# Two merges and a convolution norm as one stage of sixteen weight tiles, and a feed-forward as one written-out stage

## What is computed

```python
y_a = a.reshape(B, S, ATTN_WIDTH) @ w_proj_attn[l]
c = jax.nn.silu(layer_norm(c, conv_ln_w[l], conv_ln_b[l]))
y_b = c @ w_proj_conv[l]
g_a, g_b = jnp.split(jax.nn.sigmoid(g + gate_b[l]), 2, axis=-1)
x = x + (g_a * y_a + g_b * y_b) @ w_out[l]
h = rms_norm(x, ffn_norm_w[l])
gt, up = jnp.split(h @ w_gate_up[l], 2, axis=-1)
x = x + (jax.nn.silu(gt) * up) @ w_down[l]
```

## Time and profile before

| What | Value |
|---|---|
| three runs | 3345.98 us median, 3337.95 to 3349.73 |
| profiled execution | 3353.64 us, its span 3351.9 us (1.7 us lie around the span) |
| mean granted TensorE clock | 0.947 of 2.4 GHz |
| PE busy | 2962.7 us, 88% |
| PEld busy | 2385.1 us, 71% |
| DVE, ACT, POOL busy | 1561.5, 1235.2, 736.0 us |
| moved | 218.90 MB, mean 65 GB/s |
| median time from issue to landing, 512 KB | 3.8 us (`w_raw`) to 5.1 us (`gates`) |

### The profile page before, as it was taken

The page is one execution under the profiler, slowest core; times in us unless marked ns, Lnnn a source line. Parts: engine busy times, 40 slices in busy tenths (PEclk is TensorE's granted clock), DMA queues, the critical chain, the costliest instruction groups (busy, mean ns, idle before and its releaser), DMA issues. The chain is left out here.

```text
span 3351.9 us, 34912 instructions
## 1 busy us (share of the span) xinstructions
PE 2962.7 (88%) x13448; PEld 2385.1 (71%) x13448; DVE 1561.5 (47%) x1927; ACT 1235.2 (37%) x2024; POOL 736.0 (22%) x323
## 2 busy tenths in 40 slices
PE   6999998877778989988998999694889989998998
PEld 5787887666667767776777778482677877787786
DVE  3666552346764337777878777514322111121121
ACT  3455442334542335555554554423224111111110
POOL 2111111100002322332233323112223212121111
PEclk7999999989989989999999999897999999999999
DMA  4111122131224212121112212241330111111112
GB/s 112 44 45 57 53 68 76 30 63 40 57 79 158 84 55 68 46 65 50 54 46 65 63 53 82 106 131 58 126 126 26 44 44 38 50 50 38 44 44 76
DMA packets 239270, 218.90 MB, mean 65 GB/s; under 512 B 29304, under 2 KB 200856, under 8 KB 239128
## 3 DMA queue, kind: packets, MB, share of 16 engines
q1 hardware_dynamic: 238096, 215.41, 21.0%
q10 hardware_dynamic: 1032, 1.57, 0.3%
HBM read 156.66 MB, written 41.42 MB: 59 GB/s over the span
## 5 line engine op out<-in xcount | busy, mean ns | idle before, releaser
L179 POOL TENSOR_TENSOR w_lo<-w_raw,w_hi 128x1024 fp32r<-128x1024 f32 (+3 forms) x220 | 521.1, 2371 | 2014.1 <-ACT w_hi L171 2014.1
L171 ACT ACTIVATE w_hi<-w_raw 128x1024 fp32r<-128x1024 f32 (+3 forms) x220 | 215.3, 983 | 666.5 <-PE u_y_ps L1688 221.3
L209 PE MATMUL d_pp<-h_hi,w_hi 128*128 128x512 f32 x896 | 367.9, 411 | 32.5 <-DVE d_padded L2523 20.7
L2501 DVE SCALAR_TENSOR_TENSOR d_acc<-d_padded,vectors,d_acc 128x1024 f32<-128x1024 f32 x240 | 388.3, 1618 | 3.6
L209 PE MATMUL d_pp<-h_hi,w_lo 128*128 128x512 f32 x896 | 366.2, 409 | 0.0
L209 PE MATMUL d_pp<-h_lo,w_hi 128*128 128x512 f32 x896 | 363.4, 406 | 0.0
L209 PEld LDWEIGHTS d_pp<-h_hi,w_hi 128*128 128x128 f32 x896 | 173.2, 193 | 80.2 <-issue 25.4
L209 PE MATMUL s_pp<-h_hi,w_hi 128*128 128x512 f32 x512 | 206.8, 404 | 13.1 <-PEq L67 13.1
L2281 POOL TENSOR_TENSOR d_probs<-d_probs 128x128 f32<-128x128 f32 (+3 forms) x64 | 129.5, 2024 | 385.8 <-ACT d_probs L2397 385.8
L209 PE MATMUL s_pp<-h_hi,w_lo 128*128 128x512 f32 x512 | 205.2, 401 | 0.0
L209 PE MATMUL s_pp<-h_lo,w_hi 128*128 128x512 f32 x512 | 204.2, 399 | 0.0
(11 more groups left out here) (346 smaller groups left out, 6542.7 us busy)
## 6 DMA issues: line engine op xcount, KB each, us to landing
w_raw<-in_w_in SPq DMA_DIRECT2D x97, 512.0 KB, 3.8
w_raw<-in_w_gate_up SPq DMA_DIRECT2D x44, 512.0 KB, 3.8
w_raw<-in_w_down SPq DMA_DIRECT2D x22, 512.0 KB, 3.7
gates<-s_gate SPq DMA_DIRECT2D x16, 512.0 KB, 5.1
f_gate<-gates SPq DMA_DIRECT2D x16, 512.0 KB, 4.8
w_raw<-in_w_out SPq DMA_DIRECT2D x16, 512.0 KB, 3.9
w_raw<-in_w_proj SPq DMA_DIRECT2D x16, 512.0 KB, 4.8
x_tok_in<-in_x SPq DMA_DIRECT2D x8, 512.0 KB, 9.0
```

Of the source, the lines that this page charges most:

```text
L171: act.activation(self.hi[:, s, 0:chunks, :], self.raw[:, s, 0:chunks, :], ACT.Copy).then_inc(self.rounded[s], 1)
L179: pool.tensor_tensor(self.lo[:, s, 0:chunks, :], self.raw[:, s, 0:chunks, :], f32(self.hi[:, s, 0:chunks, :]), ALU.subtract).then_inc(self ...
L209: mm = pe.matmul(halves(ps)[h], w[:, k, :], x[:, k, h * HALF:(h + 1) * HALF], start=(k == 0 and r == 0), stop=(k == chunks - 1 and r == 2))
L2501: dve.scalar_tensor_tensor(out=acc[:, :], in0=x, scalar=wt, in1=acc[:, :], op0=ALU.mult, op1=ALU.add).then_inc(c["taps"], 1)
```

## The change

`merge`, `project_out`, `conv_norm` and the old `feed_forward` go; two new functions come. Their cores:

```diff
+def merge_branches(nc, ring, w_proj, heads_dram, conv_dram, gates_dram, gate_bias, y_hi, y_lo, c_hi, c_lo, x, merged_dram,
+                   ln_w, ln_b, ones, eps, ahead):
+    TILES = 2 * KC
...
+            def load_gate(t):
+                m = t % KC
+                sp.dma_start(gate[:, t % 2, :], gates_dram[t // KC][m * P:(m + 1) * P, :]).then_inc(gate_loaded[t % 2], 16)
+            def load_prior(m):
+                sp.wait_ge(c["low"], m + 1)
+                sp.dma_start(x[:, m, :], merged_dram[m * P:(m + 1) * P, :]).then_inc(prior_loaded[m], 16)
             for k in range(KC):
+                sp.dma_start(f32(c_lo[:, k, :]), heads_dram[k * P:(k + 1) * P, :]).then_inc(heads_loaded[k], 16)
+            for t in range(2):
+                load_gate(t)
+            for k in range(KC):
+                sp.dma_start(x[:, k, :], conv_dram[k * P:(k + 1) * P, :]).then_inc(conv_loaded[k], 16)
+            for t in range(min(ring.first(TILES)), TILES + 3):
+                if t < TILES:
+                    m = t % KC
+                    at = m * P + (D if t < KC else 0)
+                    ring.load(sp, 0, TILES, t, (w_proj[:, at:at + P], 0))
+                if t == TILES:
+                    ring.load_ahead(sp)
+                u = t - 3
+                if 0 <= u < KC:
+                    sp.wait_ge(c["multiplied"], u + 1)
+                    sp.dma_start(merged_dram[u * P:(u + 1) * P, :], gate[:, u % 2, :]).then_inc(stored[u % 2], 16)
+                    sp.wait_ge(stored[u % 2], 16 * (u // 2 + 1))
+                if u >= KC:
+                    sp.wait_ge(c["merged"], u - KC + 1)
+                if u >= 0 and u + 2 < TILES:
+                    load_gate(u + 2)
+                if u in (5, 7):
+                    for m in range(4):
+                        load_prior(m + (4 if u == 7 else 0))
...
+            def add_square(k):
+                pool.wait_ge(c["squared"], k + 1)
+                if k >= 2:
+                    pool.wait_ge(c["square_sum"], k - 1)
+                pool.tensor_tensor(stat[:, :], stat[:, :], square[:, k % 2, :], ALU.add).then_inc(c["square_sum"], 1)
+            def low(k):
+                pool.wait_ge(c["rounded"], k + 1)
+                pool.tensor_tensor(c_lo[:, k, :], x[:, k, :], f32(c_hi[:, k, :]), ALU.subtract).then_inc(c["low"], 1)
+            for t in ring.first(TILES):
+                ring.subtract(pool, 0, TILES, t)
+                if t in (3, 4):
+                    for k in range(1 if t == 3 else 4, 4 if t == 3 else KC):
+                        add_square(k)
+                if t in (6, 7):
+                    for k in range(4):
+                        low(k + (4 if t == 7 else 0))
+            ring.subtract_ahead(pool)
...
+            for k in range(KC):
+                act.wait_ge(heads_loaded[k], 16)
+                act.activation(y_hi[:, k, :], f32(c_lo[:, k, :]), ACT.Copy).then_inc(c["y_round"], 1)
+            for t in ring.first():
+                ring.round(act, 0, TILES, t)
+            for t in range(TILES):
+                gate_sigmoid(t)
+                if t + 2 < TILES:
+                    ring.round(act, 0, TILES, t + 2)
+                if t in (1, 2):
+                    for k in range(4):
+                        square_of(k + (4 if t == 2 else 0))
+                if t == 3:
+                    invert()
+                if t in (4, 5):
+                    for k in range(4 * (t - 4), 4 * (t - 4) + 4):
+                        sigmoid_of(k)
+                        if k % 4:
+                            round_c(k - 1)
+                    round_c(4 * (t - 4) + 3)
+            ring.round_ahead(act)
...
+            for k in range(1, KC):
+                dve.wait_ge(conv_loaded[k], 16)
+                if k == 1:
+                    dve.wait_ge(conv_loaded[0], 16)
+                else:
+                    dve.wait_ge(c["mean_sum"], k - 1)
+                dve.tensor_tensor(stat[:, :], x[:, 0, :] if k == 1 else stat[:, :], x[:, k, :],
+                                  ALU.add).then_inc(c["mean_sum"], 1)
+            for t in range(TILES):
+                multiply(t)
+                if t >= KC:
+                    merge(t - KC)
+                if t in (1, 2):
+                    for k in range(4):
+                        centre(k + (4 if t == 2 else 0))
+                if t in (4, 5):
+                    for k in range(4):
+                        scale(4 * (t - 4) + k)
+                    for k in range(4):
+                        product(4 * (t - 4) + k)
         @block.tensor
         def _(pe):
+            def add_over_rows(total, counted):
                 for h in range(2):
+                    mm = pe.matmul(halves(total)[h], ones[:, :], stat[:, h * HALF:(h + 1) * HALF], start=True, stop=True)
+                mm.then_inc(counted, 1)
+            for t in range(TILES):
+                ring.ready(pe, 0, TILES, t)
+                if t >= 2:
+                    pe.wait_ge(c["multiplied"], t - 1)
+                hi, lo = (y_hi, y_lo) if t < KC else (c_hi, c_lo)
+                for k in range(KC):
+                    if t % KC == 0:
+                        pe.wait_ge(c["y_split" if t < KC else "low"], k + 1)
+                    project(pe, ring, t, KC, hi, lo, y_ps[t % 2], 6 * k, 6 * k + 6)
+                if t == 1:
+                    pe.wait_ge(c["mean_sum"], KC - 1)
+                    add_over_rows(sum1, c["summed"])
+                if t == 3:
+                    pe.wait_ge(c["square_sum"], KC - 1)
+                    add_over_rows(sum2, c["squares_summed"])
...
+def feed_forward(nc, ring, w_gate_up, w_down, groups, h_hi, h_lo, a_hi, a_lo, x_tok, out_dram):
+    stream, at_tile = [], {}
+    f0 = 0
+    for g, n in enumerate(groups):
+        stream += [(what, f) for f in range(f0, f0 + n) for what in ("gate", "up")]
+        stream += [("down", (g, t)) for t in range(n)]
+        f0 += n
+    for t, item in enumerate(stream):
+        at_tile[item] = t
+    TILES = len(stream)
...
+        banks = mem.ps("f_banks", [P, TB * HALF])
+        g_ps = [banks[:, (4 * s) * HALF:(4 * s + 2) * HALF] for s in range(2)]
+        u_ps = [banks[:, (4 * s + 2) * HALF:(4 * s + 4) * HALF] for s in range(2)]
+        y_ps = [banks[:, b * HALF:(b + 1) * HALF] for b in range(TB)]
...
+            act.preload_act_table_set("sigmoid_and_others")
+            for t in ring.first():
+                ring.round(act, 0, TILES, t)
+            for t, (what, n) in enumerate(stream):
+                if what == "gate":
+                    sigmoid_of(n)
+                if t + 2 < TILES:
+                    ring.round(act, 0, TILES, t + 2)
+                if what == "up":
+                    round_a(n)
...
+            def add(g, n, b):
+                x = x_tok[:, b, cols(n)]
+                if b < TB - 1:
+                    dve.wait_ge(c["summed"], (2 * g + n) * (TB - 1) + b + 1)
+                else:
+                    dve.wait_ge(*ring.done(0, TILES, at_tile["down", (g, (n + 1) * (groups[g] // 2) - 1)]))
+                if g:
+                    dve.wait_ge(c["added"], ROUND * (g - 1) + n * TB + b + 1)
+                dve.tensor_tensor(x, y_ps[b], x, ALU.add).then_inc(c["added"], 1)
+            for t, (what, n) in enumerate(stream):
+                if what == "gate":
+                    silu_of(n)
+                if what == "up":
+                    product_of(n)
+                    low_a(n)
+                if what == "down":
+                    g, j = n
+                    half, last = divmod(j, groups[g] // 2)
+                    if last == groups[g] // 2 - 1:
+                        for b in range(TB):
+                            add(g, half, b)
...
+            def bank_free(f):
+                g = group_of(f)
+                k = f - first_f[g]
+                if g and k < 2:
+                    pe.wait_ge(c["added"], ROUND * (g - 1) + TB + 4 * (k + 1))
+                elif f >= 2:
+                    pe.wait_ge(c["product"], f - 1)
+            def down(t, g, j):
+                n, at = divmod(j, groups[g] // 2)
+                w_hi, w_lo = (x[:, t % SLOTS].rearrange("p c n -> p (c n)") for x in (ring.hi, ring.lo))
+                for b in range(TB):
+                    if at == 0:
+                        if n:
+                            pe.wait_ge(c["added"], ROUND * g + b + 1)
+                        elif b % 4 == 0:
+                            pe.wait_ge(c["product"], first_f[g] + groups[g] - 1 + b // 4)
+                    for i in range(2):
+                        k = 2 * at + i
+                        if n == 0 and b == 0:
+                            pe.wait_ge(c["low"], first_f[g] + k + 1)
+                        for r, (y, ww) in enumerate(((a_hi, w_hi), (a_lo, w_hi), (a_hi, w_lo))):
+                            mm = pe.matmul(y_ps[b], y[:, k, b * P:(b + 1) * P], ww[:, i * HALF:(i + 1) * HALF],
```

(72 more changed lines are left out.)

450 lines of the change are left out of this document (111 added, 339 removed).

## The result

The changed kernel takes 3228.88 us (median of 4 executions, 3226.61 to 3230.41), the kernel before 3347.86 us (4 executions, 3337.95 to 3352.78): a ratio of 0.9645, 95% interval 0.963 to 0.9659, 119.0 us less. Timed again later (5 executions against 9) it was 3224.72 us against 3351.27 us, ratio 0.9626 (0.9612 to 0.9639), 126.6 us less. The profiled execution took 3226.61 us.

A forecast was written before the change was run, and what follows sets the result against it. PE was taken to bound both stretches, with holes at stage seams and slow clock behind them. Savings of 77.5 us (merges and norm) and 47.8 (feed-forward) made 125 us, giving 3222 us, range 3203 to 3243.

The forecast's parts named there:

- Feed-forward: Five seams between six blocks vanish with no new exposed wait: 36.4 us of holes plus 11.4 of clock, 47.8 us saved.
- Entry: Start of the merges: PE waits for one split part at a time, first matmul at 2169.5 us instead of 2180.2.
- Weight tile 2: In the merges, queued behind eight conv loads: lands a little after 2191 us, ready at 2194.6, before PE needs it at 2195.3.
- Squares: Behind tile 3, PE waits 2.5 us for POOL's last square addition; clock loss taken as none, at worst 1.7 us.
- The norm's second half: Between tiles 4 and 8, DVE and POOL take turns: 47.9 us of work, PE stands 5.3 us before tile 7, 7.6 before tile 8.
- the 3.3 us for DVE's wait for ACT at the half: Term in the 47.9 us sum of the norm's second half: about 3.3 us where DVE waits for ACT.
- the sum of the stage: Merges and norm together: about 203 us from first to last matmul, 77.5 us saved.
- A: Norm's second half: DVE and POOL overlap after all; gain 136 us, time 3210 us; chance 0.08.
- B: Merge stage: written order holds PE longer through late weights, longer POOL operations, clock drops; gain 108, time 3238 us; chance 0.15.
- C: Tiles that leave the loops run at 10.9 us instead of 11.2; 15.6 us more gain, 3206 us; chance 0.08.
- D: Feed-forward seams keep a wait of about 4 us each, with clock behind; 30 us given back, 3251 us; chance 0.04.
- E: Slower than before: 60 tiles leaving loops burden PE's instruction stream; 3389 us at 14 us a tile; chance 0.02.

The follow-up runs named there:

- two rows a tile: Changed kernel with the norm's second half spread, two chunk rows behind each of tiles 4 to 7, POOL's weight subtraction ahead of low parts: 3214.64 us, ratio 0.9596.
- the seam wait: Changed kernel with PE waiting for the last row's low part at each of three down-projection starts: 3245.72 us, ratio 0.9683 to the kernel before.
- the low parts on DVE: Changed kernel with the norm's eight low parts subtracted by DVE and not POOL: 3219.18 us, ratio 0.9599 to the kernel before.
- the short seam wait: Changed kernel with PE waiting only for the last product at each of three down-projection starts: 3229.69 us, against 3224.72 for the changed kernel.
- all parts before the first matmul: Changed kernel with PE waiting for all eight split parts of the heads before its first matmul: 3233.99 us once, then 3232.24 against 3224.72.

## Why the prediction was right

**Feed-forward.** Predicted 47.8 us; 49.6 us in the profile, 46.9 us as a median alone. No wait took the place of the seams. The stretch is 783.0 - 733.6 = 49.4 us shorter: PE's idle time was 36.5 us of it, and its busy time fell by 12.9 us for the same matmuls, where the forecast had 11.4 us of clock.

**Entry.** Predicted a wait of about 14 us and a first matmul 5.6 us after the first load (2169.5 - 2163.95); it was 14.3 and 5.7 us. Weight tile 2, which I had called in time, made a wait of 0.8 us, and the step behind that was mis-added: heads and gates until 2179.5 and 12 us for conv make 2191.5, where I wrote 2190.5, and the weight tile's own half megabyte comes on top. It landed 2190.78 - 2161.82 = 29.0 us after the stage's first load, where the forecast had little more than 27 (timeline of ACT, after):

```profile
2190.78 1.06 ACT L171 ACTIVATE w_hi<-w_raw 128x1024 fp32r<-128x1024 f32 x1 [11.13 <-DMA w_raw<-in_w_proj]
```

**Squares.** The hole was sized 2.5 us and measured 2.8. The clock behind it I put at nothing, with 1.7 us as the worst: 17.35 - 15.7 = 1.7 us is what it cost in the profile of after. These stretches, of the profile after, start at the first matmul, behind the hole after tile 3, and at tile 8:

```profile
2167.50:2177.50 10.00, 9.96 (x34) 8.04 (x35) 7.64 (x7) 6.65 (x7) 0.00 (x0) 0.76 1.02 403
2219.00:2229.00 10.00, 9.79 (x32) 6.98 (x33) 0.00 (x0) 5.89 (x5) 2.46 (x2) 0.83 0.43 141
2278.90:2288.90 10.00, 9.99 (x31) 7.90 (x32) 0.00 (x0) 1.15 (x1) 2.27 (x1) 0.69 0.63 217
```

**The norm's second half.** The forecast had 47.9 us from the end of tile 4 to the start of tile 8, with holes of 5.3 and 7.6 us; it was 2278.9 - 2233.8 = 45.1 us, with holes of 3.8 and 6.0. The order in POOL's queue is the one that was walked (DVE's first scales and its wait at the half stand above POOL's rows, each from its engine's timeline):

```profile
2234.99 7.05 DVE L2654 SCALAR_TENSOR_TENSOR merged<-merged,vectors,mb_stat 128x1024 f32<-128x1024 f32 x4
...
2253.46 1.22 DVE L2636 TENSOR_TENSOR mb_gate<-mb_y,mb_gate 128x1024 f32<-128x1024 f32 x1 [2.17 <-ACT mb_gate L2577]
```

```profile
2244.41 11.54 POOL L2560 TENSOR_TENSOR h_lo<-merged,h_hi 128x1024 fp32r<-128x1024 f32 x4 [7.04 <-ACT h_hi L2606]
2255.91 3.32 POOL L179 TENSOR_TENSOR w_lo<-w_raw,w_hi 128x1024 fp32r<-128x1024 f32 x1
2265.08 11.47 POOL L2560 TENSOR_TENSOR h_lo<-merged,h_hi 128x1024 fp32r<-128x1024 f32 x4 [5.84 <-ACT h_hi L2606]
2276.49 4.69 POOL L179 TENSOR_TENSOR w_lo<-w_raw,w_hi 128x1024 fp32r<-128x1024 f32 x2
```

Low 0 to 3, then the subtraction of tile 7; low 4 to 7, then those of tiles 8 and 9. The per-row time was right: from the first scale (2234.99) to the last low part (2276.55), with the subtractions of weight tiles 6 and 7 in between (2.40 and 3.32 us) taken out, are 35.8 us, 4.48 us a row where I had 4.51. The three subtractions took 8.1 us, where I had 7.2. The term that was too large is the 3.3 us for DVE's wait for ACT at the half: DVE waited 2.17 us there, but POOL was at its low parts meanwhile, and the wait added nothing. The end of it is 1.1 + 35.8 + 8.1 = 45.0 us. As for the cause, the run with two rows a tile shows that the turns by themselves don't make the holes: with the lists spread, half of the 9.8 us is gone.

That the sum of the stage came out to 1.1 us (first to last matmul 203.8 us, predicted 202.7) is partly luck. The matmuls at full clock are 8 x 10.9 + 8 x 11.2 + 2 x 1.74 = 180.3 us in both. To this the forecast added 15.4 us of holes and 6.9 us of clock; measured were 13.4 us of holes, and what is left for the clock is 10.1 us. Holes 2.0 us too large stood against 3.2 us too little clock.

**The rivals.** A (DVE and POOL overlap) is refuted by the products that take 2.47 us for two alone and 5.88 us beside POOL. B (the written order holds PE longer) happened in small: 0.8 us before tile 2, and in the first profile 1.7 us of clock behind tile 3. C (tiles out of the loops are quicker) is refuted by the 22.40 us and by the 11.20 us of the convolution tiles. The Trainium skill, "Runtime: NRT & Kernel Launch", section "Instruction fetch mechanics", describes a stall at a taken branch whose target isn't in the window of the fetch. The traces show no such stall in these loops, 22.40 us with them and without; whether their branches leave that window isn't shown. D (a wait of 4 us stays at each seam) is refuted by the waits of after, and the run with the seam wait shows what it would have looked like. E (written-out code starves PE) is refuted by a feed-forward in which PE is busy for 733.6 of 733.6 us, with gate and up still at 22.40 us.

**The level.** It was 119.0 us in one set of rounds and 126.6 in another, with unchanged code before the stage that took 2161.8 us in the first profile and 2157.2 us in the second. A difference of that kind isn't in the reach of a sum over one trace.

## What to carry to other kernels

A block boundary between two stages costs more than its hole: here five holes of 4.6 to 9.1 us came with 1.5 to 3.0 us of missing work behind each, so the expected gain of joining stages is the holes and what the clock rows show behind them. When work is put under another engine's tiles, ask of each engine's in-order list whether something that the busy engine needs soon stands behind something that it needs late; the stage was 8 to 11 us shorter with the same work in another order and in smaller groups. And where two engines take turns, count their work together against the tiles that must cover it, then start it early enough: that, and the additions on the quicker engine, brought the saving to 145.9 us, where the change as given has 119.0 to 126.6.

## What I had not expected of the hardware

The same hole of 2.8 us, in the same place of the code, left the granted clock up in some executions and not in others. Of the nine profiles with that hole, the four passes behind it took 1.98 us in five (the second profile of the change, the runs with two rows a tile, with the low parts on DVE, with the short seam wait, and the first with all parts before the first matmul), and 2.87, 3.28, 3.67 and 3.78 us in the other four. Behind 1.4 us it stayed up all three times, and behind 4.8 us it was down all three times. Between the multiplications of tiles 3 and 4 this cost nothing in the five (15.7 us), 1.7 us in three of the others (17.4) and 2.9 us in one (18.6). The 3.8 us hole before tile 7, which seven of these profiles have, had a granted clock of 0.72 to 0.83 behind it in all seven. A hole of 2.8 us can't be priced from one trace of this kernel.
